# Column halves for two heads' values, and a third output projection that stands behind the fourth gates

## The reference

```
h = adaLN(RMSNorm(x)); proj = h @ w_in -> q,k,v of A; q,k,v of B; gate_a; gate_b
A = sliding-window attention (128), 8 query heads over 2 key heads, with a learned sink
    in every softmax denominator
B = block-sparse attention: 8 heads, blocks of 256, own causal block and the top 3 past ones
x = x + gt1 * ((sigmoid(gate_a) * (A @ w_o_swa) + sigmoid(gate_b) * (B @ w_o_moba)) @ w_out)
h = adaLN(RMSNorm(x));  x = x + gt2 * (relu(h @ w_up)^2 @ w_down)
```

## Time and profile before

| | |
|---|---|
| time, median of 3 runs | 2617.42 us (2616.05 to 2627.78) |
| profiled execution | 2618.83 us |
| span of its slowest core | 2616.9 us |
| spans of the eight cores | 2601.1 to 2616.9 us |
| PE busy | 2155.9 us, 82% |
| ACT busy | 1226.2 us, 47% |
| DVE busy | 1190.2 us, 45% |
| POOL busy | 278.1 us, 11% |
| mean granted clock of PE, this core | 0.925 |

### The profile page before, as it was taken

One profiled execution on the slowest core, in us unless ns is written; L12 is line 12 of the kernel. 1 busy time (PEld: TensorE's weight loads), 2 busy tenths in 40 slices (PEclk: granted clock), 3 DMA queues, 4 the chain that ended last, 5 costly groups with the idle time before them and its releaser, 6 DMA issues.

```text
span 2616.9 us, 32748 instructions; the slowest of 8 cores (2601.1 to 2616.9 us)
## 1 busy us (share of the span) xinstructions
PE 2155.9 (82%) x10633; PEld 911.2 (35%) x10840; DVE 1190.2 (45%) x2035; ACT 1226.2 (47%) x1689; POOL 278.1 (11%) x548
## 2 busy tenths in 40 slices
PE   1356676788889989999995686678889989999998
PEld 1223222232323434444442332222232334444444
DVE  1245576452522554444445677644351354444433
ACT  1445467848477431111115567776758552111122
POOL 1010031201012101010000021110102000000000
PEclk6578788899999999999997889899999999999999
DMA  9973600510102656473511020511010190403012
GB/s 200 190 138 41 97 17 17 81 33 1 33 1 44 96 87 81 65 98 40 105 65 57 17 57 9 82 16 33 1 33 1 42 144 1 65 14 52 1 49 81
DMA packets 127683, 149.26 MB, mean 57 GB/s; under 512 B 4384, under 2 KB 109088, under 8 KB 126496
## 3 DMA queue, kind: packets, MB, share of 16 engines
q0 software_dynamic: 108368, 85.14, 24.0%
q1 hardware_dynamic: 19152, 62.03, 7.3%
HBM read 205.02 MB, written 27.26 MB: 89 GB/s over the span
## 4 chain that ended last, share of the span: by engine, by line
PE 70%; ACT 11%; issue 6%; DVE 6%; DMA 5%; another core or an unknown queue 2%; POOL 0%; ACTq 0%; DVEq 0%; SPq 0%; POOLq 0%
PE PS L506 69%; ACT SB L532 7%; DMA SB<-w_ada 3%; DVE SB L563 3%; DVE SB L537 2%; ACT L532 2%; DMA SB<-xsp 1%; PE PS L514 1%; ACT SB L775 1%; ACT SB L742 1%; DMA SB<-w_in 1%; DVE SB L553 0%; DVE SB L577 0%; ACT SB L760 0%
## 5 line engine op out<-in xcount | busy, mean ns | idle before, releaser
L506 PE MATMUL PS<-SB 128*128 128x512 bf16 (+2 forms) x10361 | 2115.7, 364 | 434.4 <-ACT SB L532 132.5
L506 PEld LDWEIGHTS PS<-SB 128*128 128x128 bf16 (+1 forms) x10568 | 871.4, 99 | 1670.2 <-issue 890.7
L532 ACT ACTIVATE SB<-PS 128x512 f32<-128x512 f32 (+5 forms) x902 | 658.6, 747 | 1016.4 <-PE PS L506 990.3
L563 DVE SCALAR_TENSOR_TENSOR SB<-PS,SB 128x512 bf16<-128x512 f32 (+1 forms) x680 | 492.1, 728 | 635.9 <-ACT SB L532 384.9
L537 DVE TENSOR_TENSOR SB<-PS,SB 128x512 f32<-128x512 f32 (+3 forms) x312 | 205.2, 660 | 268.7 <-ACT SB L532 148.7
L537 DVE TENSOR_TENSOR SB<-SB 128x512 bf16<-128x512 f32 (+5 forms) x441 | 245.8, 571 | 146.2 <-ACT SB L532 126.5
L878 POOL COPY SB<-SB 128x128 bf16<-128x128 bf16 x382 | 116.0, 313 | 883.4 <-PE PS L506 730.2
L532 ACT ACTIVATE SB<-SB 128x512 f32<-128x512 f32 (+1 forms) x226 | 181.7, 805 | 29.9 <-DVE SB L537 15.4
L563 DVE SCALAR_TENSOR_TENSOR SB<-SB,PS 128x512 f32<-128x512 f32 x128 | 88.0, 688 | 219.4 <-PE PS L506 181.9
L563 DVE SCALAR_TENSOR_TENSOR SB<-SB 128x512 f32<-128x512 f32 x148 | 103.8, 727 | 63.8 <-ACT SB L532 51.3
L532 ACT ACT_TABLE_LOAD x81 | 103.9, 1283 | 31.3 <-DVE SB L537 14.6
(11 more groups left out here) (23 smaller groups left out, 161.1 us busy)
## 6 DMA issues: line engine op xcount, KB each, us to landing
SB<-w_ada POOLq DMA_DIRECT2D x48, 512.0 KB, 8.8
SB<-w_in POOLq DMA_DIRECT2D x16, 1024.0 KB, 12.7
xsp<-SB SPq DMA_DIRECT2D x8, 2048.0 KB, 9.3
SB<-xsp SPq DMA_DIRECT2D x64, 256.0 KB, 2.9
SB<-w_up POOLq DMA_DIRECT2D x16, 1024.0 KB, 11.6
SB<-w_down POOLq DMA_DIRECT2D x16, 1024.0 KB, 19.7
SB<-x SPq DMA_DIRECT2D x16, 512.0 KB, 16.3
SB<-cs SPq DMA_DIRECT2D x16, 512.0 KB, 4.5
```

The source lines that it names most:

```text
L506: ins = e.matmul(o, l_, rr, start=a, stop=b)
L532: S.add([('act', lambda e, o=out.ap, i=in_.ap: e.activation(out=o, in_=i, func=func, **kw), d)], r, out.keys)
L563: S.add([('dve', lambda e, o=out.ap, x=in0.ap, y=in1.ap: e.scalar_tensor_tensor(out=o, in0=x, scalar=a, in1=y, op0=op0, op1=op1), cost('dv ...
```

## The change

Five things are altered.

1. Values in column halves. The matmuls of the two heads now write partitions 0 to 63 and 64 to 127 of the same bank, with 64 columns of weights each. One pair has the values as weights (numerators, bank 4), a second pair a constant `ones64` (denominators, bank 5): four matmuls a chunk in place of two, and no copy on POOL. Ln, Exp and the multiplication then run once for both heads on 128x512; the sinks are added on 128x512 from a rearranged table `esk`.
2. The scheduler's model: other cost constants, 1.28 for each change of activation table, and 4.0 of virtual time against an operation that would change the table.
3. `c_stage` is split into `c_mix` and `c_out`. For slots 0 and 1 they follow each other as before. For slot 2 `c_out` is written behind `c_mix` of slot 3, which has a second `mixs`, laid over the buffers of the exponentials (bytes T0 to T0+8191; `nrm_r` and `nrm_t` of `norm` lie there too).
4. The residual is read back into `xslot(s)` itself, by two DMAs of 128x2048, which may start when the attention's result (lower half) and h (upper half) have been read for the last time.
5. `store_out` goes by feature block with a staging buffer of a whole slot; for the last slot two feature blocks at a time are written out.

The diff, cut to its core:

```diff
--- before.py
+++ after.py
@@ add / schedule @@
+TAB_SLACK = 4.0
...
-                if ready_t[i] <= t and (bi is None or (vt, i) < lst[bi]):
-                    bi = j
+                if ready_t[i] <= t:
+                    tb = ops[i]['tab']
+                    k = (vt + TAB_SLACK if tb is not None and tb != table[0] else vt, i)
+                    if bk is None or k < bk:
+                        bk, bi = k, j
...
+            if op['tab'] is not None and op['tab'] != table[0]:
+                table[0] = op['tab']
+                free[e] += 1.28
...
+TABS = {AF.Ln: 'ln', AF.Tanh: 'tanh', AF.Silu: 'silu', AF.Sin: 'sin'}
...
-        den = sb(T0 + 8192, (2, 512), F32)
+        den = [sb(T0 + 8192 + i * 2048, (512,), F32) for i in range(2)]
-        vaug = [sb(T0 + 14336 + i * 512, (2, 128), BF16) for i in range(4)]
+        ones64 = sb(T0 + 14336, (64,), BF16)
+        esk = sb(VB + 2176, (L, 4), F32)
-        mixs = sb(T0 + 18176, (8, 512), BF16)
+        mixs = [sb(T0 + 18176, (8, 512), BF16), sb(T0, (8, 512), BF16)]
-        xring = [sb(T0 + 30464 + i * 2048, (512,), F32) for i in range(2)]
...
             if eng == 'act':
-                return 0.11 + n * 0.000833
+                return 0.175 + n * 0.000833
             if eng == 'dve':
-                return 0.13 + n / 960.0 / fast
-            return 0.25 + n * (0.0022 if two else 0.001)
+                return 0.155 + n / 960.0 / fast
+            return 0.25 + n * (0.0022 if two else 0.00155)
...
-            po = ps(4, (2, 512))
-            dn = den.part(64, 128)
+            pn, pd = ps(4, (512,)), ps(5, (512,))
+            pn4, pd4 = ps(4, (4, 128)), ps(5, (4, 128))
+
+            def values(v, p_, q0, first, last):
+
+                for o, w_ in ((pn, v), (pd, lambda hf: ones64)):
+                    mms([(o[hf * 64:(hf + 1) * 64, q0:512], w_(hf), p_[:, hf, q0:512], first, last)
+                         for hf in range(2)])
...
-                    va = vaug_pair(c, 0)
...
-                    for g in range(2):
-                        mm(po[:, g], va[:, g], p_[:, g], ci == 0, ci == len(chunks) - 1)
-                d8 = SBA.view(den.off, (8, 128), F32).part(64, 128)
-                tt(d8, PSA.view(4 * 2048, (8, 128), F32).part(64, 128),
-                   _bc(esink[64:128, l * 8:l * 8 + 8], 2, 128), ALU.add)
+                    values(lambda g, c=c: vst[:, c, g * 64:(g + 1) * 64], p_, 0, ci == 0, ci == len(chunks) - 1)
+                dn = nxt('den', den)
+                d4 = SBA.view(dn.off, (4, 128), F32)
+                tt(d4, pd4, _bc(esk[:, l], 2, 128), ALU.add)
                 act(dn, dn, AF.Ln)
                 act(dn, dn, AF.Exp, scale=-1.0)
...
-                for g in range(2):
-                    tt(A[g * 64:(g + 1) * 64, 0:4, qsl], p4[0:64, g], d4[64:128, g], ALU.mult)
+                tt(A[:, 0:4, qsl], pn4, d4, ALU.mult)
...
-                    for hf in range(2):
-                        mm(po[:, hf, q0:512], va[:, hf], p_[:, hf, q0:512], j == 0, j == nch - 1)
-                act(dn, po.part(64, 128), AF.Ln)
+                    values(lambda hf, j=j, p=p: vst[:, j, 128 + p * 128 + hf * 64:192 + p * 128 + hf * 64], p_, q0,
+                           j == 0, j == nch - 1)
+                dn = nxt('den', den)
+                act(dn, pd, AF.Ln)
                 act(dn, dn, AF.Exp, scale=-1.0)
-                for hf in range(2):
-                    tt(A[hf * 64:(hf + 1) * 64, 4 + p], po[0:64, hf], den[64:128, hf], ALU.mult)
+                tt(A[:, 4 + p], pn, dn, ALU.mult)
...
-        def c_stage(l, s, w):
-            A, h, xs = ATs(s), hTs(s), xslot(s)
+        def c_mix(s, w, mx):
+            A, h = ATs(s), hTs(s)
...
+        def c_out(l, s, w, mx):
+            xs = xslot(s)
+            for h_ in range(2):
+                js = slice(h_ * 4, h_ * 4 + 4)
+                dma(xs[:, js], Raw(xsp_d[l][s][:, js], ['xsp%d_%d_%d' % (l, s, j) for j in range(h_ * 4, h_ * 4 + 4)]),
+                    'sp')
             for j in range(8):
                 q, jc = j // 4, (j % 4) * 128
-                xr = nxt('xr', xring)
-                dma(xr, Raw(xsp_d[l][s][:, j], ['xsp%d_%d_%d' % (l, s, j)]), 'sp')
                 p5 = ps(bank(), (512,))
                 for k in range(8):
-                    mm(p5, w['out'][q][:, k, jc:jc + 128], mixs[:, k], k == 0, k == 7)
-                stt(xs[:, j], p5, modv(l)[:, 16 + j:17 + j], xr, ALU.mult, ALU.add)
+                    mm(p5, w['out'][q][:, k, jc:jc + 128], mx[:, k], k == 0, k == 7)
+                stt(xs[:, j], p5, modv(l)[:, 16 + j:17 + j], xs[:, j], ALU.mult, ALU.add)
...
-        ostage = [sb(KV + 32768 + i * 4096, (8, 128), F32) for i in range(2)]
+        ostage = [sb(RW + i * 16384, (4, 8, 128), F32) for i in range(2)]
...
+            step = 8 if s < 3 else 2
+            for j in range(8):
+                pv = ps(bank(), (4, 128))
+                for tq in range(4):
+                    tr(pv[:, tq], xs[:, j, tq * 128:(tq + 1) * 128], identf)
+                cp(xo[:, :, j], pv, engs=('act', 'dve'))
+                if (j + 1) % step == 0:
+                    j0 = j + 1 - step
...
-                    c_stage(l, s - 1, WC)
-                    S.window(i0, T + c_t[s - 1][0], T + c_t[s - 1][1])
+                    t0, t1 = c_t[s - 1]
+                    c_window(c_mix, t0, t0 * 0.3 + t1 * 0.7, s - 1, WC, mixs[0])
+                    if s < 3:
+                        c_window(c_out, t0 * 0.3 + t1 * 0.7, t1, l, s - 1, WC, mixs[0])
             pool_banks[0] = list(range(8))
-            i0 = len(S.ops)
-            c_stage(l, 3, WC)
-            S.window(i0, T + c_t[3][0], T + c_t[3][1])
+            c_window(c_mix, 400, 428, 3, WC, mixs[1])
+            c_window(c_out, 428, 442, l, 2, WC, mixs[0])
+            c_window(c_out, 442, 456, l, 3, WC, mixs[1])
```

54 lines of the change are left out of this document (25 added, 29 removed).

## The result

The changed kernel took 2545.99 us in the median of four runs against 2622.6 us for the kernel before beside it; by their ratio it takes 0.9704 of the time, with a 95% interval of 0.9639 to 0.9769. A second series on another chip gave 2544.12 us and 0.9712 (0.9696 to 0.9727). So the change is worth 2.9%, some 75 us, where the forecast was 31 us and its range ended at 2555 us. The profiled execution took 2552.81 us, with a span of 2551.3 us.

The account below looks back on a forecast made before the run. Bound before slot 2 by a chain through ACT and DVE, later nearly by PE; -29 - 9 + 32 + 0 - 18 - 5 - 2 = -31 us from 2618.8 gave 2588, as median 2587 us; range 2555 to 2645 us.

Parts of the forecast that it names:

- Ends of blocks: Attention block ends: shorter ACT and DVE work saves 29 us (23 before slot 2, 6 after); ends 12 and 60.
- The clock: Slots 0 and 1: less PE idling gives back a tenth of 43 us, 5 us; ends 0 and 15.
- Table loads: ACT: fourteen fewer activation-table loads, 18 us, of which half counts: 9 us saved; ends 0 and 18.
- Changes of shape: PE in attention: 357 more array-shape changes at 0.11 us each cost 32 us, 28.6 of it from slot 2 on.
- The bad end of this term: Attention's array-shape changes at twice the price and without cover: 75 us cost.
- Residual and seam: Residual in halves: 0 us, ends -10 and +12; seam between mixing and MLP: 18 us saved, ends -3 and 20.
- the feared late landing: Seam: residuals landing last, at 35 us, would put the norm 11 us later and the gain at nothing.
- The scheduler's model: Instruction order: constants lie closer to measured durations; the resulting order could not be priced and counted nothing.
- Output: Program's end: a whole slot's staging buffer removes copies' waits for a staging buffer, 2 us saved.
- The first rival: Attention's value matmuls: column halves run one after another, +118 us, 2705 us; chance 12%.
- the second: Gains run dry: shape change 0.2 us, residuals at 35 us, block ends covered; about 2620 us, no change; chance 20%.
- The third: Column halves change shape free, or the order improves with truer constants, each some 30 us: 2556 us; chance 15%.

Follow-up runs that it names:

- e5: Kernel after with block ends as long as before (wide Ln and Exp, two multiplications, two sink additions, one denominator buffer): ratio 0.9994 to the kernel before.
- e8: Kernel before with four more unused 512-column matmuls on PE ahead of each block end in slots 0 and 1: 2634.68 us, ratio 1.0054.
- e3: Kernel before with only the attention's part: column halves, narrow block ends, no POOL copies: 2566.3 us, ratio 0.9789.
- e10: Kernel of e4, but slot 3 takes its values as before (128-column matmuls, POOL copy, long block ends): 2532.05 us, ratio 0.9658.
- e7: Kernel after with the old mixing part (residual ring, slot 2's output projection inside slot 3): 2565.43 us, ratio 0.9787.
- e1: Kernel after with the old scheduler's model (old costs, no table-change charge, no slack): 2568.55 us, ratio 0.9806.
- e2: Kernel before with only the new scheduler's model: 2626.71 us, ratio 1.003.
- e4: Kernel after with the output's staging buffer laid out by feature block (8 x 4 x 128): 2538.45 us, ratio 0.9683.
- e14: Kernel of e4 with the value copies on POOL again: 2532.99 us, ratio 0.9647.

## Why the prediction was wrong

**Ends of blocks: the step that failed.** Its durations held (629 and 688 ns for 128x512). "What is worth anything is the part that nothing covers", and for that I took PE's idle shares, 40% of 57.6 us before slot 2 and 10% behind, 29 us, and with table loads and clock 43 us. The runs give 74 us for the ends with all that hangs on them (e5). Before slot 2, where I took 23 us, they cost 58 us by e5, all of their own length: 36 us more idle time of PE and some 26 us for the lower clock. From slot 2 on, where I took 6 us, it is some 22 us. (The stages sum to 80 us, the ratio says 74.) PE's share of idle time does not say how much of a chain is exposed where the chain is the bound: PE idled because of it.

**The clock: too small by far.** 28% of 175 and 22% of 172 us ran at the lower level, 87 us; after, 8% of 134 and 6% of 126 us, 18 us. That gives back up to 34 us, where I counted a tenth of 43 us, 5 us; this is the term that was missed most in proportion. The ends alone give back some 26 us of it (e5). e8 shows that this isn't had by mere work.

**What hid the rest: work only moved.** Counted in full-speed columns, slots 0 and 1 lost 10 and 13 us of gates and output projections, which short slots no longer hold; slot 3 and the seam took them. So e3's slot 3 is 24 us longer than before with 18 us more work in it, and e5's, with long ends, 14 and 21 us shorter than after with 19 and 23 us less. A stage's gain means little without this.

**Table loads.** 82 to 68 came true, but through the ends: with the model alone they stay at 82. How much of the 74 us they are was not separated; e5 makes 84.

**Changes of shape: the price was right, its sum not isolated.** 0.10 us is the price between all three shapes (0.11 forecast), and PE's busy time in slots 2 and 3 rose by 10 and 17 us (10 to 15 forecast). From slot 2 on e3 pays 18 and 23 us a layer, 41 us for both, of which 24 us are moved work. That leaves 17 us, where the forecast was 28.6: the changes there, some 300 in e3, come to 30 us at 0.10, and the shorter ends give a part back. e10 shows that removing changes at the cost of long ends gains little. (The bad end of this term, 75 us, was miscounted: 357 changes at twice 0.11 us are 79.)

**Residual and seam: right, with some luck.** e7 gives 20 us for both, forecast 18. The seam itself did what was said: it holds 9 and 10 us more work in the same time, and in the first layer's 42 us PE waits only once, 1.8 us. The two DMAs of 1024 KB landed in 7.3 us in the median, so the feared late landing did not come. But the 20 us need the new model: with the old one (e1 against e3) the new mixing part and output lose 4 us, of which the output is a loss of 8 to 11, so that the mixing part gains only 4 to 7. The seam is as good there; slot 3 gives it back.

**The scheduler's model: counted at nothing.** Alone it is nothing or less (e2); with the new mixing part it is worth 25 us (e1), 21 of them in slot 3. Why it needs the new mixing part was not tested.

**Output: the wrong sign.** 2 us of gain forecast, 11 us of loss measured (10.1 to 21.1 us from the last addition to the end), because a buffer's size was looked at and not the range of bytes that a copy touches, which makes 8.8 us of it (e4).

The first rival (serial halves) was excluded by the pairs, the second by the price of a change, e5 and e7. The third, 2556 us with "waits of 106 us to be had", was the nearest, with 15%. Of its two ways one is false, a change of shape isn't free, and one came in part, the order (e1, 25 us); but most of the gain is the ends', which neither of them names.

The best kernels measured here are e10 (2532.05 us) and e14 (2532.99 us), 3.4 to 3.5% under the kernel before and 0.5 to 0.7% under the one after; the corrected output makes about half of that.
